# Two half-width gathers: the first 128 slots of a routed expert layer gathered apart, the first two gate/up products between the other rows

## The reference, cut to what matters

```python
top_logit, top_idx = lax.top_k(sel_logits, TOP_K_IN_GROUP)
top_w = jax.nn.softmax(top_logit, axis=-1) * g_prob[:, None]
combine_e = jnp.sum(jax.nn.one_hot(top_idx, EXPERTS_PER_GROUP) * top_w[..., None], axis=1)
...
for gi in range(N_GROUPS):
    hid = (jax.nn.silu(jnp.einsum("td,edf->tef", t, expert_w_gate[gi]))
           * jnp.einsum("td,edf->tef", t, expert_w_up[gi]))
    hid = hid * combine[:, gi, :, None].astype(hid.dtype)
    y = y + jnp.einsum("tef,efd->td", hid, expert_w_down[gi])
```

## Time and profile before

| what | value |
|---|---|
| median of 3 runs | 829.93 us (829.03 to 830.1) |
| the profiled execution | 828.89 us |
| its span, first to last instruction | 827.1 us |
| TensorE busy | 767.7 us (93%) |
| VectorE busy | 487.9 us (59%) |
| read from memory | 192.35 MB |
| mean granted TensorE clock | 0.97 |

### The profile page before, as it was taken

How to read it: one execution, slowest core, us unless ns; L and a number is a source line. 1 busy time by engine, 2 the same in 40 slices (tenths; PEclk the granted TensorE clock), 3 DMA queues, 4 the chain that set the end, 5 groups by cost and what they waited for, 6 DMA issues and landing times.

```text
span 827.1 us, 16238 instructions
## 1 busy us (share of the span) xinstructions
PE 767.7 (93%) x6690; PEld 647.9 (78%) x6690; DVE 487.9 (59%) x843; ACT 376.3 (45%) x573; POOL 49.2 (6%) x91
## 2 busy tenths in 40 slices
PE   6999999999999999999999999999999877677676
PEld 6999998999999998999998999899955443344343
DVE  4455567767676678867864255487775523323326
ACT  4556664545545556567454553474332211111124
POOL 0200032000000000110101000000001000000000
PEclk9999999999999999999999999999999979879889
DMA  8964453556556554444342233449989999999993
GB/s 281 315 210 131 145 162 106 181 175 203 167 188 202 172 185 153 160 147 154 102 154 59 98 103 103 146 159 367 420 327 419 421 421 419 422 420 421 421 420 138
DMA packets 89170, 194.34 MB, mean 235 GB/s; under 512 B 3646, under 2 KB 69537, under 8 KB 76689
## 3 DMA queue, kind: packets, MB, share of 16 engines
q1 hardware_dynamic: 86640, 186.66, 61.3%
q0 software_dynamic: 1888, 4.61, 1.8%
q10 hardware_dynamic: 576, 2.14, 0.7%
HBM read 192.35 MB, written 1.05 MB: 234 GB/s over the span
## 4 chain that ended last, share of the span: by engine, by line
PE 72%; DMA 17%; DVE 5%; ACT 2%; issue 1%; SPq 1%; ACTq 0%; DVEq 0%
DMA expert_w<-in_expert_w_up 17%; PE PG L2041 15%; PE PG L2043 14%; PE PG L2042 14%; PE PG L2646 3%; PE PM L2041 3%; PE PM L2043 3%; PE PM L2042 3%; PE PM L2676 1%; PE PM L2497 1%; ACT whi L844 1%; PE PG L2668 1%; SPq L676 1%; PE PM L2122 1%; DMA rows<-in_norm_mix 1%
## 5 line engine op out<-in xcount | busy, mean ns | idle before, releaser
L2041 PE MATMUL PG<-hT_hi,whi 128*128 128x256 f32 (+1 forms) x816 | 235.8, 289 | 0.0
L2043 PE MATMUL PG<-hT_hi,wlo 128*128 128x256 f32 (+1 forms) x816 | 230.6, 283 | 0.0
L2042 PE MATMUL PG<-hT_lo,whi 128*128 128x256 f32 (+1 forms) x816 | 230.5, 282 | 0.0
L1357 DVE TENSOR_TENSOR wlo<-raw,whi 128x2048 fp32r<-128x2048 f32 x73 | 167.2, 2291 | 65.8 <-ACT whi L844 65.7
L2041 PEld LDWEIGHTS PG<-hT_hi,whi 128*128 128x128 f32 x816 | 153.9, 189 | 6.1 <-issue 2.8
L2043 PEld LDWEIGHTS PG<-hT_hi,wlo 128*128 128x128 f32 x816 | 154.2, 189 | 0.0
L2042 PEld LDWEIGHTS PG<-hT_lo,whi 128*128 128x128 f32 x816 | 153.7, 188 | 0.2
L844 ACT ACTIVATE whi<-raw 128x2048 fp32r<-128x2048 f32 x73 | 139.4, 1910 | 21.4 <-PE PG L2043 19.1
L2646 PE MATMUL PG<-expert_w,xw 128*32 128x256 f32 x992 | 74.2, 449 | 36.8 <-DMA expert_w<-in_expert_w_up 36.8
L2646 PEld LDWEIGHTS PG<-expert_w,xw 128*32 128x32 f32 x992 | 36.7, 124 | 59.0 <-issue 47.3
L1952 DVE SCALAR_TENSOR_TENSOR y_lo<-PG,small,y_hi 128x512 fp32r<-128x512 f32 x16 | 12.0, 750 | 98.4 <-ACT y_hi L1276 98.4
(11 more groups left out here) (525 smaller groups left out, 1338.3 us busy)
## 6 DMA issues: line engine op xcount, KB each, us to landing
expert_w<-in_expert_w_gate SPq DMA_DIRECT2D x32, 1024.0 KB, 26.7
expert_w<-in_expert_w_up SPq DMA_DIRECT2D x32, 1024.0 KB, 26.8
expert_w<-in_expert_w_down SPq DMA_DIRECT2D x32, 1024.0 KB, 26.9
raw<-in_ffn_w_up SPq DMA_DIRECT2D x22, 1024.0 KB, 5.0
raw<-in_w_in SPq DMA_DIRECT2D x22, 1024.0 KB, 5.1
raw<-in_moba_w_qkv SPq DMA_DIRECT2D x12, 1024.0 KB, 6.9
raw<-in_ffn_w_down SPq DMA_DIRECT2D x11, 1024.0 KB, 4.9
raw<-in_moba_w_o SPq DMA_DIRECT2D x4, 1024.0 KB, 5.1
```

What stands on the lines that cost most here:

```text
L1357: dve.tensor_tensor(lo_of(n), raw[:, n % R, :], hi_of(n).bitcast(F32), ALU.subtract).then_inc(s_lo, 1)
L2041: pe.matmul(dst, lh, rh, start=start, stop=False, **kw)
L2042: pe.matmul(dst, lh, rl, start=False, stop=False, **kw)
L2043: return pe.matmul(dst, ll, rh, start=False, stop=stop, **kw)
```

## The change

- The gather is split by slots. The first 128 slots (FIRST) of all eight feature groups are gathered first, 32 products of 128 columns, groups 0 to 3 into PG bank 3 and 4 to 7 into PG bank 1; ScalarE evacuates the first four, VectorE the other four. The other 384 slots follow in 32 products of 384 columns into PM (and the rest of PG bank 3).
- `pick` is written in the same two parts, with the offsets and the count of the fullest expert between them.
- On TensorE the rest of the gather is cut in three: groups 0 and 1, gate/up of expert 0, groups 2 and 3, gate/up of expert 1, groups 4 to 7; then the transposes of expert 0, the token rows, expert 0's down product and the transposes of expert 1. Expert 1's window lies in a buffer of its own, `xw_second`, since `xw` lies over X's low part.
- X's low part of the second token tile is made by GpSimd, not VectorE.
- Expert 5's up matrix is asked for after the gate and up matrices of experts 6 and 7, and waits as before for all feature rows.
- ScalarE's evacuation of the token rows comes after expert 0's gate; one keep-warm product of 512 columns goes.

The diff, without the changes of semaphore names and of the path `wide`:

```diff
@@ -531,6 +531,7 @@
         pair = place("pair", [P, KD, PAIRS + SEQ], 79616)
         y_in_pad = place("y_in_pad", [P, KD, PAIRS + SEQ], 79616, F32R)
         spare = place("spare", [P, 2, D // 2], 79616)
+        xw_second = pair[:, :, PAIRS + 2 * WIN:PAIRS + 3 * WIN]
         ident_r = place("ident_r", [P, P], 19712, F32R)
         sum1, mean1, sq1 = (tiny(1) for _ in range(3))
         res_hi = place("res_hi", [P, TT, D], 79616 + 12288, F32R)
...
@@ -605,6 +606,15 @@
                 narrow()
 
         NW = SEQ // WIN
+        FIRST = 4 * WIN
+
+        def first_slots(k):
+
+            return PG[:, 3 - 2 * (k // KH), FIRST * (k % KH):FIRST * (k % KH) + FIRST]
+
+        def other_slots(k):
+
+            return PG[:, 3, FIRST:PAIRS] if k == KH else PM[:, k % (KH + 1), FIRST:PAIRS]
 
         gate_upT, result = PG[:, 2, 0:SEQ].rearrange("p (j n) -> p j n", j=2), PG[:, 3, :]
         last_result = PG[:, 0, :]
@@ -686,13 +696,14 @@
             expert_load(5, 0, 5)
             sp.wait_ge(s_logit, TT + 1)
             expert_load(4, 2, 4)
-            sp.wait_ge(s_xga, KD // 2)
-            sp.wait_ge(s_xgv, KD // 2)
-            expert_load(5, 1, 5)
             for e in range(NU, NE):
                 sp.wait_ge(s_guse, 2 * (e - NU) + 2)
                 for kind in range(2):
                     expert_load(e, kind, e % NU)
+                if e == NU + 1:
+                    sp.wait_ge(s_xga, KD)
+                    sp.wait_ge(s_xgv, KD)
+                    expert_load(NU - 1, 1, NU - 1)
                 if e > NU:
                     sp.wait_ge(s_duse, e - NU)
                     expert_load(e - 1, 2, (e - 1) % NU)
@@ -804,31 +815,39 @@
                 pool.dma_start(lnrow[:, i, :], a[name][0].partition_broadcast(P)).then_inc(s_lnrow, 16)
 
             pool.wait_ge(s_gran, G_END)
-            pool.memset(pair[:, :, PAIRS:PAIRS + SEQ], 0.0).then_inc(s_pad, 1)
+            pool.memset(pair[:, :, PAIRS:PAIRS + SEQ], 0.0).then_inc(s_padlo, 1)
+            pool.wait_ge(s_xhi3, 2)
+            pool.tensor_tensor(X_lo[1][:, :], X[:, 1, :], X_hi[1][:, :].bitcast(F32), ALU.subtract).then_inc(s_padlo, 1)
             pool.wait_ge(s_xga, KD // 2)
             pool.wait_ge(s_xgv, KD // 2)
-            pool.wait_ge(s_pad, 1)
-
-            def window(at, i2):
-                pool.tensor_copy(xw[i2][:, :, :], pair[:, :, bass.ds(at, WIN)]).then_inc(s_win, 1)
+            pool.wait_ge(s_padlo, 2)
+
+            def window(at, dst):
+                pool.tensor_copy(dst, pair[:, :, bass.ds(at, WIN)]).then_inc(s_win, 1)
+
+            def others_in():
+                pool.wait_ge(s_xga, KD)
+                pool.wait_ge(s_xgv, KD)
 
             def begins(e):
                 return pool.value_load(offi[0:1, e:e + 1] if isinstance(e, int) else offi[0:1, bass.ds(e, 1)], min_val=0, max_val=PAIRS)
 
             def narrow():
-                window(begins(1), 1)
+                window(begins(1), xw_second)
+                others_in()
                 with pool.Fori(0, NE // 2 - 1) as r:
                     for u in range(2):
...
 
...
         @block.scalar
@@ -1257,11 +1276,16 @@
             centred(1)
             rows_hi(1)
             act.preload_act_table_set("exp_and_others")
+
+            def features_in(k, c, src, count):
+                act.wait_ge(s_xg, count)
+                act.activation(pair[:, k, c], src, ACT.Identity, scale=lncol[:, 2, k:k + 1], bias=lncol[:, 3, k:k + 1]).then_inc(s_xga, 1)
+
+            for k in range(KH):
+                features_in(k, slice(0, FIRST), first_slots(k), KH)
             for k in range(0, KD, 2):
-                act.wait_ge(s_xg, k + 1)
-                act.activation(pair[:, k, 0:PAIRS], PM[:, k % 4, :], ACT.Identity, scale=lncol[:, 2, k:k + 1],
-                               bias=lncol[:, 3, k:k + 1]).then_inc(s_xga, 1)
-                if k == 0:
+                features_in(k, slice(FIRST, PAIRS), other_slots(k), KD + k + 1)
+                if k == 2:
                     act.wait_ge(s_scalar, 1)
                     act.activation(e5, d5, ACT.Exp).then_inc(s_answer, 1)
             act.preload_act_table_set("silu_and_others")
@@ -1294,8 +1318,6 @@
                         tokens_hi(NE - 1)
                     act.wait_ge(s_guse, 2 * e + 2)
                     sums_out(e % 2)
-                    if e == 0:
-                        rows_out()
                     if e > 0:
                         act.wait_ge(s_slotw, e)
                         act.wait_ge(s_duse, e)
@@ -1304,6 +1326,8 @@
                     if e > 1:
                         act.wait_ge(s_hm, e - 1)
                     gate(e % 2)
+                    if e == 0:
+                        rows_out()
                 act.wait_ge(s_slotw, NE)
                 act.wait_ge(s_duse, NE)
                 act.activation(last_y[:, 0, :], last_result, ACT.Copy, scale=slotw[(NE - 1) % 2]).then_inc(s_yhi, 1)
@@ -1868,22 +1892,37 @@
             slotpos = PG[:, 1, 0:2 * NE].rearrange("p (t n) -> p t n", t=TT)
             step(dve.tensor_tensor(of_two, M1M2, slotpos.unsqueeze(1).to_broadcast([P, 2, TT, NE]), ALU.mult))
             step(dve.tensor_reduce(pos, of_two, AX.X, ALU.add))
+
+            def picks(t, c):
+                step(dve.tensor_scalar(pick2[:, t, c], con("slots")[:, c], pos[:, 1, t, :], None, ALU.is_equal))
+                dve.scalar_tensor_tensor(pick[:, t, c], con("slots")[:, c], pos[:, 0, t, :], pick2[:, t, c], ALU.is_equal, ALU.add).then_inc(s_P, 1)
+
             for t in range(TT):
-                step(dve.tensor_scalar(pick2[:, t, :], con("slots"), pos[:, 1, t, :], None, ALU.is_equal))
-                dve.scalar_tensor_tensor(pick[:, t, :], con("slots"), pos[:, 0, t, :], pick2[:, t, :], ALU.is_equal, ALU.add).then_inc(s_P, 1)
-
-            rows_lo(1)
+                picks(t, slice(0, FIRST))
+
             dve.wait_ge(s_rank, 2)
             step(dve.tensor_copy(off, PG[:, 2, 0:NE]))
             step(dve.tensor_reduce(cmax, PG[:, 2, NE:2 * NE], AX.X, ALU.max))
             step(dve.tensor_copy(offi[0:1, 0:NE], off[0:1, :]))
             dve.tensor_copy(offi[0:1, NE:NE + 1], cmax[0:1, :]).then_inc(s_off, 1)
+            for t in range(TT):
+                picks(t, slice(FIRST, PAIRS))
+
+            def features_out(k, c, src, count):
+                dve.wait_ge(s_xg, count)
+                dve.tensor_scalar(pair[:, k, c], src, lncol[:, 2, k:k + 1], lncol[:, 3, k:k + 1], ALU.mult, ALU.add).then_inc(s_xgv, 1)
+
+            for k in range(KH, KD):
+                features_out(k, slice(0, FIRST), first_slots(k), KD)
+            others = slice(FIRST, PAIRS)
+            features_out(1, others, other_slots(1), KD + 2)
             each = [P, SEQ // WIN, NE]
             slot1 = con("slot1").unsqueeze(2).to_broadcast(each)
             within = above[:, 0:SEQ // WIN * NE].rearrange("p (w n) -> p w n", n=NE)
             step(dve.tensor_tensor(within, PG[:, 2, NE:2 * NE].unsqueeze(1).to_broadcast(each), slot1, ALU.is_ge))
             step(dve.tensor_tensor(slot_at[:, :, :], off.unsqueeze(1).to_broadcast(each), slot1, ALU.add))
             step(dve.tensor_tensor(slot_at[:, :, :], slot_at[:, :, :], within, ALU.mult))
+            features_out(3, others, other_slots(3), KD + 4)
             step(dve.tensor_scalar(of_token[:, :, 0:2].rearrange("p t (i n) -> p i t n", n=1), pos, 1.0, None, ALU.add))
 
             step(dve.tensor_reduce(gmax, groups, AX.X, ALU.max))
@@ -1891,26 +1930,19 @@
             step(dve.tensor_tensor(of_two, M1M2, experts.unsqueeze(1).to_broadcast([P, 2, TT, NE]), ALU.mult))
             step(dve.tensor_reduce(top, of_two, AX.X, ALU.add))
             dve.tensor_tensor(d5[:, :, GROUPS:5], top[:, 1, :, :], top[:, 0, :, :], ALU.subtract).then_inc(s_scalar, 1)
-
-            def features_out(k):
-                dve.wait_ge(s_xg, k + 1)
-                dve.tensor_scalar(pair[:, k, 0:PAIRS], PM[:, k % 4, :], lncol[:, 2, k:k + 1], lncol[:, 3, k:k + 1],
-                                  ALU.mult, ALU.add).then_inc(s_xgv, 1)
-
-            features_out(1)
+            for k in (5, 7):
+                features_out(k, others, other_slots(k), KD + k + 1)
             dve.wait_ge(s_answer, 1)
             step(dve.tensor_reduce(gsum, e5[:, :, 0:GROUPS], AX.X, ALU.add))
             step(dve.scalar_tensor_tensor(w1, e5[:, :, GROUPS:5], 1.0, gsum, ALU.add, ALU.mult))
             step(dve.reciprocal(w1, w1))
             step(dve.tensor_tensor(w2, w1, e5[:, :, GROUPS:5], ALU.mult))
-            features_out(3)
+
             def diagonals(t):
                 dve.tensor_tensor(diag[t][:, :, :], con("ident").unsqueeze(1).to_broadcast([P, 4, P]),
                                   of_token[:, t, :].unsqueeze(2).to_broadcast([P, 4, P]), ALU.mult).then_inc(s_diag, 1)
 
             diagonals(0)
-            features_out(5)
-            features_out(7)
             diagonals(1)
 
             def tokens_whole(t):
@@ -2607,29 +2639,35 @@
```

(66 more changed lines are left out.)

14 lines of the change are left out of this document (7 added, 7 removed).

## The result

The changed kernel takes 835.68 us, median of 5 runs (835.01 to 837.8), against 829.93 us (829.03 to 831.28, 5 runs) for the kernel before: ratio 1.0073, 95% interval 1.0058 to 1.0088, so slower by 5.75 us. The two traces are therefore 8.3 us apart, more than the medians.

What follows compares the result with a forecast made beforehand. Weight transfers at 421 GB/s, plus time with none asked for, bound the kernel. Expert 8's gate matrix flowing at 628.8 instead of 623.1 adds 5.7 us to 829.93, giving 835.6 us; range 830.6 to 837.2.

Steps and rivals of the forecast that it cites:

- the dry ring: Weight buffers' queue around routing: no transfers asked for until buffers free up; first issue 606.46 before, 609.4 forecast.
- Expert 8's gate matrix decides: After the dip: the change is worth the shift in when this matrix begins to flow, 623.1 to 628.8, +5.7 us.
- its transfer rule: Queue after the dip: expert 8's gate matrix flows at first issue + 1.7 us + six transfers, 14.9 us.
- A gathering product costs 0.247 us at any width: TensorE's gather: strided weight loads set the price; 64 products take 15.8 us in place of 7.9.
- The rival with the low price: Gather: narrow products at 0.118 us; 829.4 us with GpSimd's blocking, 827.4 without; chance 18%.
- GpSimd blocks VectorE: At VectorE's marks of two experts, 593.14: held by GpSimd's 2.5 us subtraction; first products at 597.2 against 595.15 unblocked.
- The first issues at 609.4: After first gather, branch, 8 products and first gate/up: first two issues at 609.4 instead of 606.46 and 607.6.
- Last feature row, first sums, token rows, third gate/up product: Chain behind the gathers: ends at 618.2, 619.1, 621.75 and 627.1, the last 11.9 us late.
- The second rule, +2.8 over the first: Expert 8's gate matrix flows 1.7 us after the third gate/up product ends, queue dry: 628.8 against 626.0.
- the first rule: Expert 8's gate matrix flows at first issue + 1.7 + 14.9 us: 626.0, or +2.9 us.

Runs made afterwards that it cites:

- e4: Changed kernel with expert 5's up matrix asked for in its old place, ahead of experts 6 and 7: 842.18 us, ratio 1.0142.
- e9: Kernel before with each of its 32 gathering products of 512 columns cut into 128 and 384 columns, nothing else: 835.91 us, ratio 1.0071.
- e2: Changed kernel with X's high and low parts written group by group, so weight columns lie side by side: 833.09 us, ratio 1.0040.
- e6: Kernel before with only X's low part of the second token tile made by GpSimd: 832.17 us, ratio 1.0023.
- e8: Changed kernel with 13 instead of 3 small keep-warm products ahead of the gather: 836.27 us, ratio 1.0068.
- e7: Changed kernel with ScalarE's table load and VectorE's four share instructions moved ahead of their last two feature rows: 835.86 us, ratio 1.0070.
- e12: Changed kernel with X's low part back on VectorE, and table load and shares ahead of the last feature rows: 835.17 us, ratio 1.0053.
- e1: Changed kernel with the second tile's low part of X back on VectorE, after its narrow marks: 835.04 us, ratio 1.0066.
- e3: Kernel before with X's two parts laid out so that weight columns lie side by side: 834.60 us, ratio 1.0053.

## Why the prediction was right

It said 835.6 us; 835.68 was measured. That they agree to 0.1 us is luck: the five runs spread over 2.8 us, and the profiled execution, for which the prediction's sum gave 834.6, took 837.17. The mechanism can be checked more closely than the time. Six transfers, 6.29 MB, are to flow between the dry ring and expert 8's gate matrix; the prediction has them done at 623.1 before and at 628.8 after. Summed from the transfers in the traces it is 623.05 and 628.65. The windows from 606 and from 611, where the queue is still empty, to these moments (6.27 and 6.28 MB by the rounded rates), first the kernel before, then the changed kernel:

```profile
606.00:623.05 17.05, 15.19 (x175) 7.54 (x168) 12.70 (x30) 5.24 (x15) 2.27 (x5) 1.00 0.93 368
```

```profile
611.00:628.65 17.65, 13.45 (x106) 8.85 (x105) 10.32 (x26) 6.79 (x15) 1.54 (x3) 1.00 0.95 356
```

Of the 8.3 us between the two profiled executions, 0.5 lie ahead of the change (592.00 and 592.49), 5.1 more have come up by expert 8's gate matrix, 1.2 in the thin places behind it, and 1.6 behind the last 5 MB. The prediction had 5.7 for the second of these and nothing for the other three. By its own steps:

- *Expert 8's gate matrix decides.* Right. The prediction's difference in flow, 5.7 us, stands against 10.8 - 4.7 = 6.1 us' worth more missing bytes, and e4 bears out its transfer rule at a size where scatter doesn't blur it. What it didn't have: it called the transfers dense from the first issue + 1.7 us on (1.44 in this trace), but thin places follow where few transfers are in the queue (309 GB/s at 615 to 618, 359 at 630 to 635). That the short queue is their cause was not tested.
- *A gathering product costs 0.247 us at any width.* Right, 0.24 in the changed kernel and in e9, where this alone costs 5.9 us. The rival with the low price, 18%, has its 0.115 only with columns side by side (e2).
- *GpSimd blocks VectorE.* Right, though not at the marks of experts that I named but one instruction later: 2.22 us for a subtraction of 32 elements. Alone it costs 2.2 us by the medians, 1.9 by the ratio, its share of the clock included (e6). The Trainium skill, "SBUF — State Buffer", "Who interferes with whom", says that a VectorE instruction with two SBUF inputs and a GpSimd one that reads SBUF lock each other out for the whole instruction; these rows agree. The first product came at 597.54 (597.2 said), in an execution that came to the routing 0.5 later.
- *The first issues at 609.4.* 610.11, 0.7 late, of which 0.5 is the later start of this execution. The one mis-sized term is this: the eight 384-column products, with 0.2 for the branch, were put at 2.2 us and took 2.8 (605.26 to 608.08), 0.32 apart at the half clock; a narrow gather of 7.7 instead of 7.9 us and a shorter gate/up product took part of it back. The prediction had not considered the clock at all, and had called the removed keep-warm product worth nothing; e8, with ten small fillers more, did not save it.
- *Last feature row, first sums, token rows, third gate/up product.* 618.2, 619.1, 621.75 and 627.1 said; 618.9, 619.6, 622.3 and 627.3 measured. TensorE's wait for the first sums was 1.6 said, 1.50 measured. VectorE's two diagonals were "done at some 620.5" by the prediction and ended at 621.11. The token rows were not held by it: their four products took 1.98 us (620.36 to 622.34), as in the kernel before. But it leaves them no room to come 1.28 us earlier, so e7 had to shorten both chains.
- *The second rule, +2.8 over the first.* By the first rule the measured first issue, 610.11, gives 610.11 + 1.7 + 14.9 = 626.7; the bytes were 1.9 later, at 628.65. So the trace bears the second rule out in the main, but e7 and e12 didn't confirm its worth in time, and this stays open.

The two costly parts alone, e9 and e6, add up to 5.9 + 2.2 = 8.1 us, more than the whole change's 5.75. That would mean that the change's idea, two gate/up products between the other rows and the sixth up matrix behind them, gives some 2 us back; but the intervals of the three ratios also allow a gain of nothing, so this is an indication and not shown.

What stays open is the cause of the scatter ahead of the routing and behind the last 5 MB, and with it why shortening the chains behind the last feature row (e7) or the start of the gather (e1) moved the medians so little. Not tried was a layout of X that its own writers leave side by side, which would give e2's price without e2's doubled copies.

## What to carry to other kernels

Before a product is cut in two, see what bounds it: where the weight load does, the halves cost twice the whole, and a narrow one costs as much as a wide one. When the end is set by a full ring of buffers, count the bytes missing around the dip and ask of each edit when the next transfers can be asked for; here one late wait at the head of that queue cost about as much as the whole change (e4). Before two traces are compared, find an instruction ahead of the edit and see by how much they differ there already. And an operation given to an idle engine is not free if it locks a busy one out: look for the shortest instruction beside it that suddenly takes microseconds.

## What the runs showed of the hardware

- The weight load of 128 columns taken with a step of 32 bytes takes 0.34 us, the same at a granted clock of 1.00 and of 0.50 (TensorE at 2.4 and 1.2 GHz); starts 0.24 apart for narrow products. Side by side it is 0.19 with starts 0.115 apart at the full clock, and 0.33 with starts 0.21 apart at the half.
- The granted clock fell to 0.50 during rows of narrow products, with 2.2 us of idle time ahead (changed kernel), 0.4 us (e1) or none (e8), and stayed at 1.00 where narrow and wide ones alternated (e9). Narrow products were not needed for it: in e6 a wait of 1.9 us was followed by 0.57 (600 to 603) beside 512-column products, and in e3 waits of 0.51 and 1.26 us by starts 0.43 apart.
- ScalarE's copy of 1024 columns takes 1.06 us in order, 2.07 with a 32-byte step on the reading side and 1.98 with a 512-byte step on the writing side; VectorE's subtraction goes from 1.22 to 2.2 (e2).
- A GpSimd subtraction on 1024 columns holds a VectorE instruction that starts beside it until its own end: 2.22 us for 0.19 (changed kernel, e6), and 2.68 for 0.29 where the VectorE instruction reads one matrix (e2).
